# Moving waits and small steps inside a chunk-ordered fp32 decoder kernel

## The reference, cut to what matters

```python
for layer in range(2):
    u = rms_norm(h, norm_mix)
    z, xbc, dt_raw, q, k, v, g_ssd, g_attn = split(u @ w_in)
    y_ssd = ssd_mixer(z, xbc, dt_raw, ...)       # conv4 + silu, softplus dt, chunked state scan
    y_attn = dilated_attention_mixer(q, k, v)    # rope on q, k; 3 patterns, 8 kv heads
    merged = sigmoid(g_ssd) * (y_ssd @ w_ssd) + sigmoid(g_attn) * (y_attn @ w_attn)
    h = h + merged @ w_out
    gate, up = split(rms_norm(h, norm_ffn) @ w_gate_up)
    h = h + (silu(gate) * up) @ w_down
```

## Time and profile before

| what | value |
|---|---|
| median of three runs | 1586.74 us |
| profiled execution | 1586.74 us, span 1584.9 us |
| TensorE busy | 1562.8 us, 99% of the span |
| VectorE busy | 1021.6 us, 64% |
| ScalarE busy | 871.1 us, 55% |
| GpSimd busy | 27.9 us, 2% |
| chain that ended last | TensorE 87%, VectorE 5%, issue 4%, ScalarE 4% |
| TensorE's granted clock | full, but for 3.4 us at the start of layer 1 |
| waits of TensorE's weight loads for ScalarE's L1264 | 6.8 us in all, 12 places, longest 0.6 us |
| waits of ScalarE's L1099 for TensorE | 338.4 us, 122 places |

### The profile page before, as it was taken

How to read it: one execution, slowest core, us unless ns; L and a number is a source line. 1 busy time by engine, 2 the same in 40 slices (tenths; PEclk the granted TensorE clock), 3 DMA queues, 4 the chain that set the end, 5 groups by cost and what they waited for, 6 DMA issues and landing times.

```text
span 1584.9 us, 21096 instructions
## 1 busy us (share of the span) xinstructions
PE 1562.8 (99%) x8014; PEld 1321.1 (83%) x8014; DVE 1021.6 (64%) x1290; ACT 871.1 (55%) x1073; POOL 27.9 (2%) x20
## 2 busy tenths in 40 slices
PE   7999999999999999999999999999999999999998
PEld 6888888888888888988888888888888888888887
DVE  5978876655665454787886665666544575677565
ACT  5756666554454442676666645435444365656564
POOL 0000000000000000000000000000000000000000
PEclk9999999999999999999999999999999999999999
DMA  6434434444355554444434434445546574446431
GB/s 254 169 137 156 158 139 158 158 160 158 132 212 189 179 186 173 161 160 160 147 143 145 178 136 160 156 166 188 186 158 214 198 251 161 140 159 220 166 137 76
DMA packets 39161, 264.80 MB, mean 167 GB/s; under 512 B 4343, under 2 KB 5016, under 8 KB 8344
## 3 DMA queue, kind: packets, MB, share of 16 engines
q1 hardware_dynamic: 37816, 260.63, 46.1%
q10 hardware_dynamic: 1248, 2.83, 0.5%
HBM read 261.61 MB, written 1.84 MB: 166 GB/s over the span
## 4 chain that ended last, share of the span: by engine, by line
PE 87%; DVE 5%; issue 4%; ACT 4%; DMA 0%; DVEq 0%; ACTq 0%
PE ps L573 23%; PE ps L571 23%; PE ps L572 23%; PE ps L576 5%; PE ps L849 2%; PE ps L851 2%; PE ps L850 2%; ACT w_high L1099 2%; PE ps L703 2%; DVE w_low L1534 1%; DVE conv L1621 1%; DVE scratch L1806 1%; PE ps L757 1%; PE ps L676 0%; PE ps L678 0%
## 5 line engine op out<-in xcount | busy, mean ns | idle before, releaser
L1534 DVE TENSOR_TENSOR w_low<-w_raw,w_high 128x2048 fp32r<-128x2048 f32 (+1 forms) x248 | 559.7, 2257 | 439.5 <-ACT w_high L1099 364.2
L1099 ACT ACTIVATE w_high<-w_raw 128x2048 fp32r<-128x2048 f32 (+1 forms) x198 | 372.8, 1883 | 351.1 <-PE ps L573 338.4
L571 PE MATMUL ps<-w_high,u_high 128*128 128x512 f32 x1376 | 550.3, 400 | 0.5 <-DVE w_low L1534 0.5
L573 PE MATMUL ps<-w_high,u_low 128*128 128x512 f32 x1376 | 537.8, 391 | 0.0
L572 PE MATMUL ps<-w_low,u_high 128*128 128x512 f32 x1376 | 536.7, 390 | 0.0
L573 PEld LDWEIGHTS ps<-w_high,u_low 128*128 128x128 f32 x1376 | 258.4, 188 | 55.1
L571 PEld LDWEIGHTS ps<-w_high,u_high 128*128 128x128 f32 x1376 | 258.8, 188 | 53.6 <-issue 1.9
L572 PEld LDWEIGHTS ps<-w_low,u_high 128*128 128x128 f32 x1376 | 259.0, 188 | 52.2 <-issue 1.9
L571 PE MATMUL ps<-w_high,b_high 128*128 128x512 f32 x384 | 152.6, 398 | 0.0
L573 PE MATMUL ps<-w_high,b_low 128*128 128x512 f32 x384 | 150.1, 391 | 0.0
L572 PE MATMUL ps<-w_low,b_high 128*128 128x512 f32 x384 | 149.6, 390 | 0.0
(11 more groups left out here) (234 smaller groups left out, 1412.9 us busy)
## 6 DMA issues: line engine op xcount, KB each, us to landing
w_raw<-in_stream SPq DMA_DIRECT2D x240, 1024.0 KB, 4.7
w_raw<-in_stream SPq DMA_DIRECT2D x8, 512.0 KB, 3.3
h<-in_x SPq DMA_DIRECT2D x4, 256.0 KB, 6.1
ple_gain<-in_ple_g ACTq DMA_DIRECT2D x2, 512.0 KB, 5.7
out<-h SPq DMA_DIRECT2D x4, 256.0 KB, 2.0
par<-in_pars SPq DMA_DIRECT2D x3, 269.0 KB, 4.9
scratch<-in_const SPq DMA_DIRECT2D x1, 768.0 KB, 7.0
rev<-scratch ACTq DMA_DIRECT2D x1, 768.0 KB, 3.6
```

The costliest lines, as they stand in the source:

```text
L571: nc.tensor.matmul(o, hi, whi, start=start, stop=False, **kw)
L573: return nc.tensor.matmul(o, lo, whi, start=False, stop=stop, **kw)
L1099: nc.scalar.activation(WH[:, c % RING, 0:n], W[:, c % RING, 0:n], ACT.Copy).then_inc(high_ready, 1)
L1534: return nc.vector.tensor_tensor(out=o, in0=a, in1=b, op=op)
```

## The change

It rearranges steps and leaves every computation as it is:
- TensorE's cumulative sums go from ahead of chunk 7 to ahead of chunk 6.
- ScalarE's two decay exponentials go from c 11 to c 9, ahead of the first tap. VectorE's `dt_out` goes from c 11 to c 10.
- On VectorE the normalisation of a head (c s + 3) goes from ahead of the chunk's `split_low` to behind it and behind rope; the low part of a head's output (c s + 5) goes behind both.
- VectorE's rope doesn't wait any more for its own earlier rope.
- At the feed-forward norm, squares and sum go from c 66 to c 65, root and inverse from c 67 to c 66.

```diff
@@ tensor: before(l, c)
-                if c == 7:
+                if c == 6:
                     pe.wait_ge(ones_ready, 1)
                     pe.wait_ge(adt_ready.sem, adt_ready.at(l, 1))
@@ scalar
-                    if c == 11:
+                    if c == 9:
                         act.wait_ge(cum_out.sem, cum_out.at(l, 1))
                         nc.scalar.activation(dec_in, acum[:, HEADS:2 * HEADS], ACT.Exp)
                         nc.scalar.activation(dec_out, acum[:, 2 * HEADS:3 * HEADS], ACT.Exp).then_inc(decays.sem, 1)
@@ scalar
                     if c == GU_AT + 1:
                         ffn_to_high(l, 3)
-                    if c == GU_AT + 2:
                         act.wait_ge(ffn_h.sem, ffn_h.at(l, 4))
                         squared(2)
                         squared(3).then_inc(ffn_squared.sem, 1)
-                    if c == GU_AT + 3:
+                    if c == GU_AT + 2:
                         act.wait_ge(ffn_sum.sem, ffn_sum.at(l, 1))
@@ vector: ahead of split_low
-                    for n, s in enumerate(HEAD_AT):
-                        if c == s + 3:
-                            dve.wait_ge(att_exp.sem, att_exp.at(l, n + 1))
...
-                            nc.vector.tensor_scalar(sc0[:, 0:P], sc0[:, 0:P], azi[:, 0:1], None, ALU.mult).then_inc(att_p.sem, 1)
                     split_low(l, c)
-                    for n, s in enumerate(HEAD_AT):
-                        if c == s + 5:
-                            dve.wait_ge(o_high.sem, o_high.at(l, n + 1))
-                            tt(bL[:, 16 + n, :], ps[:, 6, 0:S], bH[:, 16 + n, :].bitcast(F32), ALU.subtract).then_inc(o_ready.sem, 1)
@@ vector: c == 10, then the x tiles at c == 2 * i + 7
                         ins.then_inc(cb_masked.sem, 1)
+                        dve.wait_ge(decays.sem, decays.at(l, 1))
+                        chain.then(dve, tt(dt_out, dt[:, 0:HEADS], dec_out, ALU.mult))
...
                             if g:
                                 dve.wait_ge(state_ps.sem, state_ps.at(l, g))
-                            else:
-                                dve.wait_ge(decays.sem, decays.at(l, 1))
-                                chain.then(dve, tt(dt_out, dt[:, 0:HEADS], dec_out, ALU.mult))
@@ vector: rope
                             dve.wait_ge(tile_out.sem, tile_out.at(l, ACT_TILE[i]))
-                            if n:
-                                dve.wait_ge(roped.sem, roped.at(l, n))
@@ vector: behind rope
+                    for n, s in enumerate(HEAD_AT):
+                        if c == s + 3:
+                            dve.wait_ge(att_exp.sem, att_exp.at(l, n + 1))
...
+                            nc.vector.tensor_scalar(sc0[:, 0:P], sc0[:, 0:P], azi[:, 0:1], None, ALU.mult).then_inc(att_p.sem, 1)
                     for n, s in enumerate(HEAD_AT):
                         if c == s + 2:
...
+                        if c == s + 5:
+                            dve.wait_ge(o_high.sem, o_high.at(l, n + 1))
+                            tt(bL[:, 16 + n, :], ps[:, 6, 0:S], bH[:, 16 + n, :].bitcast(F32), ALU.subtract).then_inc(o_ready.sem, 1)
```

More of the change, by code:

```diff
@@ L1680, in _ @@
                             tt(y[:, 1, :], y[:, 1, :], yoff, ALU.add).then_inc(ssd_y.sem, 1)
-                    for n, s in enumerate(HEAD_AT):
-                        if c == s + 3:
-                            dve.wait_ge(att_exp.sem, att_exp.at(l, n + 1))
-                            tt(sc1[:, 0:S], sc1[:, 0:S], sc1[:, S:2 * S], ALU.add)
-                            tt(sc0[:, 0:P], sc0[:, 0:P], sc0[:, P:2 * P], ALU.add)
-                            chain.then(dve, nc.vector.reciprocal(azi, az))
-                            tt(sc1[:, 0:S], sc1[:, 0:S], sc1[:, 2 * S:3 * S], ALU.add)
-                            chain.then(dve, tt(sc0[:, 0:P], sc0[:, 0:P], sc0[:, 2 * P:3 * P], ALU.add))
-                            nc.vector.tensor_scalar(sc1[:, 0:S], sc1[:, 0:S], azi[:, 1:2], None, ALU.mult)
-                            nc.vector.tensor_scalar(sc0[:, 0:P], sc0[:, 0:P], azi[:, 0:1], None, ALU.mult).then_inc(att_p.sem, 1)
                     split_low(l, c)
-                    for n, s in enumerate(HEAD_AT):
-                        if c == s + 5:
-                            dve.wait_ge(o_high.sem, o_high.at(l, n + 1))
-                            tt(bL[:, 16 + n, :], ps[:, 6, 0:S], bH[:, 16 + n, :].bitcast(F32), ALU.subtract).then_inc(o_ready.sem, 1)
                     if c == 5:
@@ L1798, in _ @@
                             ins.then_inc(roped.sem, 1)
+                    for n, s in enumerate(HEAD_AT):
+                        if c == s + 3:
+                            dve.wait_ge(att_exp.sem, att_exp.at(l, n + 1))
+                            tt(sc1[:, 0:S], sc1[:, 0:S], sc1[:, S:2 * S], ALU.add)
+                            tt(sc0[:, 0:P], sc0[:, 0:P], sc0[:, P:2 * P], ALU.add)
+                            chain.then(dve, nc.vector.reciprocal(azi, az))
+                            tt(sc1[:, 0:S], sc1[:, 0:S], sc1[:, 2 * S:3 * S], ALU.add)
+                            chain.then(dve, tt(sc0[:, 0:P], sc0[:, 0:P], sc0[:, 2 * P:3 * P], ALU.add))
+                            nc.vector.tensor_scalar(sc1[:, 0:S], sc1[:, 0:S], azi[:, 1:2], None, ALU.mult)
+                            nc.vector.tensor_scalar(sc0[:, 0:P], sc0[:, 0:P], azi[:, 0:1], None, ALU.mult).then_inc(att_p.sem, 1)
                     for n, s in enumerate(HEAD_AT):
```

## The result

The changed kernel took 1606.15 us, the median of four runs (1606.06 to 1606.17), against 1586.57 for four runs of the kernel before (1585.42 to 1589.53). The ratio is 1.0121, with a 95% interval of 1.0109 to 1.0134: slower by 19.6 us. The forecast was 1600.4, in a range up to 1603.8. Direction and places were right; six microseconds were missing.

A forecast was written before the change was run, and what follows sets the result against it. TensorE, busy 99% of the span, was taken to bound the kernel. Stage 1 2.5, attention 3.35 and feed-forward 1.0 make 6.85 a layer, 13.7 in two: 1586.74 + 13.7 = 1600.4 us, 8-in-10 range 1597.0 to 1603.8.

The forecast's parts named there:

- The sums, +0.15: Stage 1, TensorE: a new stall of 0.82 ahead of chunk 6 replaces the old one ahead of chunk 8, net +0.15.
- the first tap, +2.5: Stage 1, ScalarE: tap behind the decays at 67.80, so L1217 makes TensorE late at chunk 9; +2.5, the 0.15 included.
- Attention, 3.35 a layer: VectorE's new order in attention makes TensorE wait: 1.35 + 0.7 + 0.3 + 1.0 = 3.35 us in a layer.
- 1.64 - 0.29 = 1.35: Scores of chunk 42: TensorE stalls 1.64 for the second head's output; the next L757 wait gives 0.29 back.
- Swallowed by the next L757 wait, so 0: Heads 2, 6 and 7, only normalisation ahead of the output: stalls of 0.1 to 0.2, counted as 0.
- Chunk 56: Normalisation at c 57 goes ahead of the gating, so TensorE waits at chunk 56: +1.0.
- I take 0.15 each: Attention, c 39 and c 47: rope passes in front; at least 0, at most 1.46, taken as 0.15 each.
- Feed-forward, +1.0: Feed-forward norm: squares ahead of chunk 66's high part make its low part late for TensorE, +1.0 in a layer.
- The clock, a rival with 0.18: New stall ahead of chunk 9 makes TensorE's clock fall, 1.7 each: one fall 1602.1, two 1603.8; chance 0.18.
- Table load: Rival: activation table loads at c 9 and c 10 run behind the wait, 2 x 1.28 a layer, 1605.5; chance 0.04.
- waits that don't bind: Rival: unseen slack meets the stalls at chunks 44, 46 and 66, 2 x 2.0 missing, 1596.4; chance 0.11.
- not slower: Rival: VectorE takes the sums early, chunk 8's stall is won and attention's are swallowed, 1585.4; chance 0.05.

The follow-up runs named there:

- `one_decays`: The kernel before with only ScalarE's decay exponentials at c 9 ahead of the first tap and VectorE's `dt_out` at c 10: 1593.51 against 1587.79 us.
- `one_cum`: The kernel before with only TensorE's cumulative sums moved from ahead of chunk 7 to ahead of chunk 6: 1587.83 against 1587.79 us.
- `best1`: The kernel before, VectorE taking the sums ahead of chunk 9's low part, ScalarE's L1264 and L1267 ahead of the next head's exponential: 1582.56 against 1587.02 us.
- `best2`: `best1` with ScalarE's copies L1214 and L1217 at c 10 also ahead of Silu: 1580.58 against 1589.52 us for the kernel before.
- `one_attention`: The kernel before with only VectorE's new order of low part, rope, normalisation and output, without rope's wait for rope: 1600.50 against 1587.79 us.

## Why the prediction was right in kind and wrong in size

- *The sums, +0.15, and the first tap, +2.5: right.* The tap was put at 67.80 and came at 67.39, the turn ahead of chunk 9 at 77.91 and came at 77.58, in a trace that is 0.37 early at chunk 5. `one_decays` has 2.46 for it, `one_cum` 0.14, and with the tap first the 2.4 are gone. No table load was on the path.
- *Attention, 3.35 a layer: right places, too small.* This is the step that failed: the term was mis-sized. It measured 5.0 in each layer, so 3.3 of the missing six lie here. Two things were left out. The chain on VectorE was moved along with TensorE's landmark, but it hangs on the ring, which keeps a delay that TensorE gets back at the next L757. And the heads with only a normalisation in front were put at 0 without being worked out. Piece by piece, in layer 0:
  - At chunk 42 I had 1.64 - 0.29 = 1.35, and the stall was 2.14 with a net of 1.8 behind the next L757. I started VectorE's chain at the 301.13 of the earlier trace rows, moved along with TensorE. But the low part starts at 305.67, 4.54 later, while TensorE arrives at the scores only 4.13 later (its own landmark). Why the 0.41 more, ScalarE's rows say:

```profile
302.62 0.47 ACT L1264 ACTIVATE scratch<-ps 128x384 f32<-128x384 f32 x1
...
303.72 1.92 ACT L1099 ACTIVATE w_high<-w_raw 128x2048 fp32r<-128x2048 f32 x1 [0.63 <-PE ps L573]
```

  Before, the high part followed L1264 without a pause; now it waits 0.63 for the end of chunk 40. That chunk was held up by its own new stall of 0.62 ahead of the scores and ended 4.55 later than before, which is the 4.54 of the low part. The L757 wait then gave 0.4 back to TensorE, but not to the ring. The other 0.09 is the start: `b_low` ends at 311.21 + 0.42 = 311.63 and L737 starts at 311.77, 0.14 later, not the 0.05 that I had read at chunk 8. With both, 1.64 + 0.41 + 0.09 = 2.14.
  - "Swallowed by the next L757 wait, so 0", for the heads with only a normalisation in front: not so. Chunks 40 and 54 became 0.70 and 0.66 later, L757 gave back 0.4 of each, and 0.29 and 0.24 stayed. Only at chunk 52 all of it came back. I had put the stalls at 0.1 to 0.2 without working them out.
  - Chunk 56: 1.26, and 0.21 at the transposes in front of it, for 1.0. Most of what the 1.26 has too much is the ring again. The gating starts 9.57 later than the 400.22 of the earlier trace rows:

```profile
409.79 2.35 DVE L1533 TENSOR_TENSOR scratch<-scratch,ps 128x1024 f32<-128x1024 f32 x2
```

  Less the normalisation's 1.87 that is 7.70, and chunk 54 was 7.72 late, while TensorE arrives at chunk 56 only 7.51 late.
  - "I take 0.15 each" for c 39 and 47: about 0.1 and 0.28. Chunk 44: 0.87 for 0.7.
- *Feed-forward, +1.0: 1.13 and 1.17.* The same 0.1 of late start.
- *The clock, a rival with 0.18: it happened,* with nearly the 1.7 that it was given for each fall: in this trace two new falls, +1.58 and +1.7, and one old fall less, which with the wait behind it makes the -0.86. Against it I had set that TensorE is dense on both sides. That was no argument: a stall of two microseconds between dense stretches is just where it fell.
- *Table load, waits that don't bind, not slower:* none of them happened. That VectorE would take the sums early was excluded rightly; `best1` had to move the taking itself to get there. That rival, like the bound of 4.8 us for what can be won, counts the stall at chunk 8 at its full 0.67, and `best1` shows that the slack at chunk 9 gives only 0.09 of it.

The sum of the corrections between the two traces: +0.1 for stage 1, +3.3 attention, +0.3 feed-forward, +3.3 for the two new falls, -0.9 and -0.4 at the starts of the layers, on 13.7, is 19.4 of 19.5. Between the medians, 19.6 apart, the stalls are 17.4 of it. The 2.2 left are not settled: the interval of the ratio is 17.3 to 21.3 us, and the four executions behind the median of 1606.15 had a mean clock of 0.999, so at most one fall each, where the profiled one had two (0.998) and took 0.3 more. At equal mean clock the two kernels are 18.6 (0.999) and 16.9 (0.998) apart, on either side of the stalls. What stays open too is why the clock falls behind one stall and not behind its twin, below.

## What to carry to other kernels

Before a step is moved across another, count the slack of everything hung on that number, in the unit of the ring: a stall of TensorE delays the splits three chunks on, so a small stall that seems to be given back at once still makes the next one longer. Put behind a long wait only what is needed later than the wait ends, and look for the gain in the instruction order just ahead of the waiting one (take the sums before the long low part), not in offering the input sooner. A step that is released sooner also starts its follower sooner, perhaps beside an instruction that it slows, as GpSimd's did in `best2`. And a new stall of about two microseconds on TensorE should be priced with a chance of a fall of the clock beside it: here 1.6 to 1.7 us, behind 5 of 12 such stalls.

## What the runs showed of the hardware

- The granted clock fell to the 1.2 GHz level for 3.4 us within 1.3 us behind the end of single idle times of TensorE of about 2 us, in a stretch that was dense otherwise. It cost 1.58 to 1.75 each time. But the same stall brought a fall in one trace and none in another: at chunk 9 in layer 0 of the changed kernel, not in its layer 1, and not in `one_decays` or with rope last, where it was 2.2 to 2.4 as well; at chunk 42 in layer 1 of the changed kernel, in both layers of `one_attention`, in layer 0 alone with the tap first. In the filled kernels, where TensorE had matmuls of no use in these places, no fall came there. What decides between such twins was not found.
- Falls also differ between executions of one and the same kernel, so a trace shows one draw. Of 42 executions of the kernel before, the 6 with a mean clock of 1.000 took 1585.3 to 1585.9 us, the 19 with 0.999 took 1586.3 to 1589.0, the 17 with 0.998 took 1589.3 to 1590.0. Of 20 of the changed kernel, 12 had 0.999 (1604.8 to 1606.2), 4 had 0.998 (1606.2 to 1606.5) and 4 had 0.997 (1607.5 to 1608.2). `best2`, without the stalls, had 1.000 four times out of four, within 0.4 us. The fall at the start of layer 1 is there in 8 of the 14 traces.
- A VectorE instruction took longer beside one of GpSimd. In `best2` a tap of 128 x 256 that reads `xpad` and `conv` took 2.12 beside GpSimd's `decay_rows` (2.02) and 0.48 otherwise, in both layers. In the kernel before, the six rope instructions that take 1.03 at 303.67 took 2.73 at 139.05, beside the same GpSimd instruction at 139.41. But at 74.91 it ran beside two VectorE instructions that read `ps`, and these took 0.69 and 0.68, as they do in `best2` without it.
- An activation table load runs ahead of the semaphore wait of the instruction it serves (1.28 at 64.11 and at 71.28), so it is free where ScalarE waits anyway. Where it does not, the switch costs the 1.28 and no more (469.36).
- TensorE started 0.05 after its releaser's end at chunk 8 before, but 0.14 after it at L737 in the changed kernel. Whether the number of semaphores in the wait makes the difference was not tried.
- The 128 x 128 float32 matmuls used as fillers took 0.23 each and left two records each (ten gave x20), twice what I had counted.
